# Inverse of a chunk's triangular matrix: its 16x16 blocks on VectorE by way of DRAM, decay rows by DMA, and four gate pairs ahead of the merge

## The reference, cut to what matters

```python
diff = G[..., :, None] - G[..., None, :]            # G: cumulated log decay
decay = jnp.where(tri_incl, jnp.exp(jnp.where(tri_incl, diff, 0.0)), 0.0)
a_mat = jnp.where(tri_strict, beta[..., None] * kk * decay, 0.0)
sol = lax.linalg.triangular_solve(a_mat + eye, rhs, left_side=True, lower=True, unit_diagonal=True)
...
s = (einsum(q, k) * scale + cum[:, :, q0:q1, None] - cum[:, :, None, :q1])   # forgetting attention
...
merged = sigmoid(gate_a) * y_a + sigmoid(gate_b) * y_b
```

## Time and profile before

| | |
|---|---|
| median of 3 runs | 2027.18 us (2027.12 to 2027.74) |
| the profiled execution | 2026.91 us |
| its span | 2025.1 us, 28477 instructions |
| mean granted TensorE clock | 0.993 of full |
| TensorE busy (matmul) | 1969.9 us (97%) |
| TensorE weight load | 1607.0 us (79%) |
| VectorE | 904.0 us (45%) |
| ScalarE | 692.0 us (34%) |
| GpSimd | 929.7 us (46%) |
| DMA queue of SP | 171.21 MB, 26.1% of 16 engines |

### The profile page before, as it was taken

The page is one execution under the profiler, slowest core; times in us unless marked ns, Lnnn a source line. Parts: engine busy times, 40 slices in busy tenths (PEclk is TensorE's granted clock), DMA queues, the critical chain, the costliest instruction groups (busy, mean ns, idle before and its releaser), DMA issues.

```text
span 2025.1 us, 28477 instructions
## 1 busy us (share of the span) xinstructions
PE 1969.9 (97%) x10484; PEld 1607.0 (79%) x10484; DVE 904.0 (45%) x1566; ACT 692.0 (34%) x1390; POOL 929.7 (46%) x711
## 2 busy tenths in 40 slices
PE   6999999999989999999999999999999999999997
PEld 5788778877768888888888788888778888888886
DVE  4766776677642122221212356667432235335143
ACT  4343333433342223332324344455332232222122
POOL 3443354434424456445445534234244555546455
PEclk9999999999999999999999999999999999999998
DMA  5111111111113252323233322121232323323232
GB/s 188 63 63 62 52 41 62 62 52 52 63 42 114 83 180 91 106 91 98 93 97 101 107 92 73 48 75 64 63 126 93 104 82 102 108 84 96 93 103 73
DMA packets 50645, 174.25 MB, mean 86 GB/s; under 512 B 6544, under 2 KB 7312, under 8 KB 50320
## 3 DMA queue, kind: packets, MB, share of 16 engines
q1 hardware_dynamic: 50432, 171.21, 26.1%
q10 hardware_dynamic: 144, 2.10, 0.3%
HBM read 169.09 MB, written 4.19 MB: 86 GB/s over the span
## 4 chain that ended last, share of the span: by engine, by line
PE 91%; DVE 5%; issue 2%; ACT 1%; DMA 0%; POOL 0%; DVEq 0%; POOLq 0%; ACTq 0%; SPq 0%
PE bank L284 26%; PE bank L286 26%; PE bank L285 26%; PE bank L1491 2%; PE bank L1480 2%; PE bank L1474 2%; PE bank L950 1%; PE bank L1671 1%; PE bank L934 1%; PE bank L1658 1%; PE bank L920 1%; DVE branch_a_lo L546 0%; DVE decay_b L1969 0%; DVE branch_b_lo L546 0%; PE bank L1557 0%
## 5 line engine op out<-in xcount | busy, mean ns | idle before, releaser
L273 POOL TENSOR_TENSOR slab_lo<-slab_raw,slab_hi 128x512 fp32r<-128x512 f32 x604 | 822.4, 1387 | 995.9 <-ACT slab_hi L266 995.8
L284 PE MATMUL bank<-u_hi,slab_hi 128*128 128x512 f32 x1584 | 656.8, 415 | 18.3 <-POOL slab_lo L273 13.5
L286 PE MATMUL bank<-u_hi,slab_lo 128*128 128x512 f32 x1584 | 620.9, 392 | 0.0
L285 PE MATMUL bank<-u_lo,slab_hi 128*128 128x512 f32 x1584 | 619.6, 391 | 0.0
L266 ACT CAST slab_hi<-slab_raw 128x1024 fp32r<-128x1024 f32 x302 | 313.8, 1045 | 230.8 <-PE bank L286 229.7
L284 PEld LDWEIGHTS bank<-u_hi,slab_hi 128*128 128x128 f32 x1584 | 299.2, 189 | 79.9 <-issue 18.3
L286 PEld LDWEIGHTS bank<-u_hi,slab_lo 128*128 128x128 f32 x1584 | 298.3, 188 | 64.9
L285 PEld LDWEIGHTS bank<-u_lo,slab_hi 128*128 128x128 f32 x1584 | 299.6, 189 | 53.7 <-issue 1.7
L284 PE MATMUL bank<-hidden_hi,slab_hi 128*128 128x512 f32 x432 | 168.4, 390 | 0.3
L286 PE MATMUL bank<-hidden_hi,slab_lo 128*128 128x512 f32 x432 | 168.1, 389 | 0.0
L285 PE MATMUL bank<-hidden_lo,slab_hi 128*128 128x512 f32 x432 | 168.1, 389 | 0.0
(11 more groups left out here) (336 smaller groups left out, 2669.6 us busy)
## 6 DMA issues: line engine op xcount, KB each, us to landing
slab_raw<-slabs SPq DMA_DIRECT2D x302, 512.0 KB, 3.4
residual<-x_t SPq DMA_DIRECT2D x2, 1024.0 KB, 7.1
x_tok<-x SPq DMA_DIRECT2D x1, 2048.0 KB, 13.5
residual<-x_t SPq DMA_DIRECT2D x1, 2048.0 KB, 8.8
residual_store<-residual SPq DMA_DIRECT2D x1, 2048.0 KB, 8.8
residual<-residual_store ACTq DMA_DIRECT2D x1, 2048.0 KB, 8.2
out_t<-residual SPq DMA_DIRECT2D x8, 256.0 KB, 2.1
cos_ret<-cos_r SPq DMA_DIRECT2D x1, 256.0 KB, 4.0
```

The costliest lines, as they stand in the source:

```text
L273: ins = pool.tensor_tensor(w_lo[s][:, ks, :], raw[s][:, ks, :], w_hi[s][:, ks, :].bitcast(F32), ALU.subtract)
L284: pe.matmul(bank, w_hi[s][:, k, :], x_hi[:, k, :], start=first, stop=False)
L285: pe.matmul(bank, w_hi[s][:, k, :], x_lo[:, k, :], start=False, stop=False)
L286: mm = pe.matmul(bank, w_lo[s][:, k, :], x_hi[:, k, :], start=False, stop=last)
```

## The change

The levels b = 1, 2, 4 and 8 leave TensorE. a_t is now the whole product of 128x512; SP stores it to DRAM with a row pitch such that the 32 diagonal blocks of 16x16 can be read back one to a partition (`blocks_out`). A new token `zb` on VectorE inverts the blocks there, in 19 instructions on 32 partitions (`product` multiplies elementwise with broadcast operands and sums). SP stores the result, and after that reads it back as zi (`blocks_back`), which `xt` transposes. `Y0`/`X0` to `Y2`/`X2` are what were levels 4 to 6. GpSimd makes the two masks left in one token `am`, now 128x512 each. `zb` stands after `vp`, and `kpd` waits for it, since k_rhs is its scratch. `gr` and `cr` go: the table of cumulated sums is transposed once in the first round (`gates3`), stored to DRAM, and SP loads two rows for each head, broadcast to all partitions (`load_rows`). AHEAD becomes 4: LAST holds eight gate slabs, six spread between the tokens and two behind them, and the split of the branches (`br0`..`br7`) stands between the parts of those two. Homes of the eight gate tiles move to the residual's place and others.

```diff
-LEVELS = 7
+SB = 16
+SUBS = T // SB
+DIAG = SB * (SB + 1)
+LEVELS = (16, 32)
 HB, QB = 64, 32
 HW = NT * HB
 SCALE = float(P) ** -0.5
 SLOTS = 4
-DVE_STEPS, LATE_STEPS = 26, 10
+DVE_STEPS, LATE_STEPS = 38, 10
 LEAD = 2
 
-AHEAD = 2
+AHEAD, SPREAD = 4, 6
...
+    row_store = nc.dram_tensor("row_store", (2 * HEADS * NT, P), F32, kind="Internal").ap()
+    row_view = row_store.rearrange("(a h n) t -> h a (n t)", a=2, h=HEADS)
+    pitch = (P // SB) * SB * (P + 1)
+    a_store, z_store = [nc.dram_tensor(f"{x}_blocks_store", (NT * pitch,), F32, kind="Internal").ap() for x in "az"]
+
+    def tiles_in(store):
+        return store.rearrange("(n x) -> n x", n=NT)[:, 0:P * P].rearrange("n (p c) -> p n c", p=P)
+
+    def blocks_in(store):
+        return store.rearrange("(q x) -> q x", q=SUBS)[:, 0:SB * P].rearrange("q (i w) -> q i w", w=P)[:, :, 0:SB]
...
+        g_line, cumr = rows[:, 0, :], rows[:, 1, :]
...
+        gates_ahead = [g[:] for g in gate_home] + [q[:, 3:3 + T] for q in rawq] + [a_out[:], raw_fq[:]]
...
-        ORDER = """gr cr fvt s0.0 dif s0.1 colb fr bd s0.2 eg fk s0.3 kk th3 s0.4 S0 s0.5 z0 s0.6 xt sl3 E0 s0.7 dm qk s1.0 Y1
-                   e0 s1.1 tv P0 s1.2 vp s1.3 s1.4 X1 kpd T0 S1 s1.5 E1 s1.6 Y2 qd P1 s1.7 O0 s2.0 X2 e1 T1 S2 s2.1
-                   E2 cv0.0 s2.2 Y3 O1 s2.3 cv0.1 P2 X3 s2.4 cv0.2 s2.5 Y4 T2 s2.6 S3 cv0.3 s2.7 X4 E3 s3.0 e2 O2 s3.1 Y5
-                   th0 P3 s3.2 cv1.0 s3.3 X5 T3 cv1.1 s3.4 sl0 s3.5 Y6 O3 cv1.2 s3.6 tq s3.7 X6 cv1.3 s4.0 e3 s4.1 vk
+        ORDER = """fvt s0.0 dif s0.1 colb fr bd s0.2 eg fk s0.3 kk th3 s0.4 S0 s0.5 am s0.6 sl3 E0 s0.7 dm qk s1.0
+                   e0 s1.1 tv P0 s1.2 vp zb s1.3 s1.4 kpd T0 S1 s1.5 E1 s1.6 qd P1 s1.7 O0 s2.0 e1 T1 S2 s2.1
+                   E2 cv0.0 s2.2 O1 s2.3 xt cv0.1 P2 s2.4 cv0.2 s2.5 Y0 T2 s2.6 S3 cv0.3 s2.7 X0 E3 s3.0 e2 O2 s3.1 Y1
+                   th0 P3 s3.2 cv1.0 s3.3 X1 T3 cv1.1 s3.4 sl0 s3.5 Y2 O3 cv1.2 s3.6 tq s3.7 X2 cv1.3 s4.0 e3 s4.1 vk
...
-                if (places.index(n) + 1) * 2 * AHEAD * KT // len(places) > part:
+                if (places.index(n) + 1) * SPREAD * KT // len(places) > part:
...
+        LAST.append(f"e{SPREAD - 1}")
+        for g in range((2 * AHEAD - SPREAD) * KT):
+            j, t = SPREAD + g // KT, g % KT
+            LAST.append(f"s{j}.{t}")
+            if t == 0 and j > SPREAD:
+                LAST.append(f"e{j - 1}")
+            if g % 2 == 0:
+                LAST.append(f"br{g // 2}")
...
+        def branch_lo(dve, rnd, k):
+            if k == 0:
+                if rnd == 0:
+                    dve.wait_ge(sem("oa"), HEADS)
+                    dve.wait_ge(sem("ob"), HEADS)
+                else:
+                    dve.wait_ge(sem("ret_out"), 2 * RET_HEADS)
+                    dve.wait_ge(sem("att_out"), 2 * RET_HEADS + 1)
+                dve.tensor_scalar(ms_col[:, 0:1], ms_col[:, 0:1], 1.0, None, ALU.mult).then_inc(sem("branches_done"), 1)
+            for n, (hi, lo, br) in enumerate(((a_hi, a_lo, br_a), (b_hi, b_lo, br_b))):
+                dve.wait_ge(sem("br_hi"), (rnd * KT + k) * 2 + n + 1)
+                dve.tensor_tensor(lo[:, k, :], br[:, k, :], hi[:, k, :].bitcast(F32), ALU.subtract)\
+                    .then_inc(sem("br_lo"), 1)
...
+            def blocks_out(c):
+                sp.wait_ge(sem("masked"), c + 1)
+                sp.wait_ge(sem("blocks_moved"), 80 * c + 32)
+                sp.dma_start(tiles_in(a_store), c4(a_t[:])).then_inc(sem("blocks_moved"), 16)
+                sp.wait_ge(sem("blocks_moved"), 80 * c + 48)
+                sp.dma_start(sub_u[:, 0:SB * SB].rearrange("q (i j) -> q i j", j=SB), blocks_in(a_store))\
+                    .then_inc(sem("blocks_moved"), 16)
+
+            def blocks_back(c):
+                sp.wait_ge(sem("sub_z"), c + 1)
+                sp.dma_start(blocks_in(z_store), sub_z[:, 0:SB * SB].rearrange("q (i j) -> q i j", j=SB))\
+                    .then_inc(sem("blocks_moved"), 16)
+                sp.wait_ge(sem("blocks_moved"), 80 * c + 80)
+                for r in (0, HB):
+                    sp.dma_start(c4(zi[r:r + HB, :]), tiles_in(z_store)[r:r + HB, :, r:r + HB])\
+                        .then_inc(sem("blocks_moved"), 16)
+
+            sp.wait_ge(sem("mhalf"), 1)
+            sp.dma_start(z_store[0:P * T].rearrange("(p t) -> p t", t=T), zeros[:]).then_inc(sem("blocks_moved"), 16)
+            sp.dma_start(z_store[P * T:].rearrange("(p t) -> p t", t=T), zeros[0:1, :]).then_inc(sem("blocks_moved"), 16)
+
+            def load_rows(i):
+                sp.wait_ge(sem("exp"), 4 * i)
+                sp.dma_start(rows[:], row_view[bass.ds(i, 1), :, :].to_broadcast([P, 2, T])).then_inc(sem("rows_landed"), 16)
...
+                            if ph is ph_heads and j == 5:
+                                blocks_out(i - 1)
+                            if ph is ph_heads and j == 6:
+                                blocks_back(i - 1)
+                                load_rows(i)
...
-                def gr():
-                    pe.wait_ge(sem("head_cols"), c + 1)
-                    rows_of(bB, h_small[:, Q_GCUM, :]).then_inc(sem("g_row_ps"), 1)
-
-                def cr():
-                    pe.wait_ge(sem("sq"), 4 * c + 4)
-                    rows_of(bD, h_small[:, Q_LFC, :]).then_inc(sem("cum_row_ps"), 1)
+                def gates3():
+                    pe.wait_ge(sem("gl_cols"), 1)
+                    pe.transpose(bA[0:2 * HEADS * NT, 0:P], gl_cols[:], ident[:]).then_inc(sem("gl_ps"), 1)
...
-                    if l < LEVELS - 1:
-                        pe.wait_ge(sem("atm"), 6 * c + l + 1)
-                    if l == 1:
-                        pe.wait_ge(sem("x0"), c + 1)
-                    else:
-                        pe.wait_ge(sem("x_new"), 5 * c + l - 1)
-                    if l < LEVELS - 1:
-                        quads(bA, atm[l % 2], xi).then_inc(sem("y_ps"), 1)
-                        return
+                    if l < len(LEVELS):
+                        pe.wait_ge(sem("atm"), 2 * c + l + 1)
+                    pe.wait_ge(sem("x_new"), 3 * c + l + 1)
                     pe.sem_inc(sem("level_begun"), 1)
                     for n in range(NT):
                         q = slice(n * HB, (n + 1) * HB)
-                        mm = pe.matmul(bA[HI, q], a_off[LO, q], xi[LO, q], start=True, stop=True)
+                        if l < len(LEVELS):
+                            for r in (LO, HI):
+                                mm = pe.matmul(bA[r, q], atm[l][r, n * P + r.start:n * P + r.stop], xi[r, q],
+                                               start=True, stop=True)
+                        else:
+                            mm = pe.matmul(bA[HI, q], a_t[LO, n * P + HB:(n + 1) * P], xi[LO, q], start=True, stop=True)
                     mm.then_inc(sem("y_ps"), 1)
...
+                    pe.wait_ge(sem("y"), 3 * c + l + 1)
+                    if l == 0:
                         pe.wait_ge(sem("v_rhs"), c + 1)
-                    if l > 1:
-                        pe.wait_ge(sem("z_new"), 6 * c + l - 1)
-                    if l < LEVELS - 1:
-                        quads(bC, yi, zi).then_inc(sem("zy_ps"), 1)
-                        return
+                    else:
+                        pe.wait_ge(sem("z_new"), 3 * c + l)
                     pe.sem_inc(sem("level_begun"), 1)
                     for n in range(NT):
-                        mm = pe.matmul(bC[LO, n * HB:(n + 1) * HB], yi[HI, n * HB:(n + 1) * HB],
-                                       zf[HI, n * P + HB:(n + 1) * P], start=True, stop=True)
+                        q = slice(n * HB, (n + 1) * HB)
+                        if l < len(LEVELS):
+                            for r in (LO, HI):
+                                mm = pe.matmul(bC[r, q], yi[r, q], zi[r, q], start=True, stop=True)
+                        else:
+                            mm = pe.matmul(bC[LO, q], yi[HI, q], zf[HI, n * P + HB:(n + 1) * P], start=True, stop=True)
                     mm.then_inc(sem("zy_ps"), 1)
...
-                    dve.wait_ge(sem("g_row_ps"), c + 1)
+                    dve.wait_ge(sem("rows_landed"), 16 * c + 16)
                     for n in range(NT):
                         q = slice(n * P, (n + 1) * P)
-                        ins = dve.tensor_scalar(dt_[:, q], bB[:, q], h_small[:, Q_GCUM, n:n + 1], 0.0, ALU.subtract,
+                        ins = dve.tensor_scalar(dt_[:, q], g_line[:, q], h_small[:, Q_GCUM, n:n + 1], 0.0, ALU.subtract,
                                                 ALU.min)
...
                 def kpd():
                     dve.wait_ge(sem("sq_ps"), 4 * c + S_K + 1)
+                    dve.wait_ge(sem("sub_z"), c + 1)
...
-                    for out_, p0, c0 in ((a_c, 0, 0), (a_c, HB, HB), (a_off, 0, HB)):
-                        p_, c_ = slice(p0, p0 + HB), slice(c0, c0 + HB)
```

(69 more changed lines are left out.)

139 lines of the change are left out of this document (69 added, 70 removed).

## The result

The changed kernel takes 2039.05 us (median of 5 runs), the kernel before 2027.12 in the runs beside it: a ratio of 1.0056 (95% interval 1.0041 to 1.0071), slower by 0.6%. One of the five took 3252.16 us at a mean granted clock of 0.557; the ratio leaves it out, and the median of the other four is 2038.1. The profiled execution took 2037.12 us.

The account below looks back on a forecast made before the run. TensorE, busy for 97% of the span, was taken to bound the kernel. Seven rounds at +1.85 us (+13.0) and the last round's -4.9 gave +8.1 on the median 2027.18: 2035.3 us, range 2008 to 2057.

Parts of the forecast that it names:

- leaves TensorE, a round: TensorE's queue: six inverse stages a head (4.6 us) and eight transposes (0.89 us) go, together 5.5 us a round.
- (a): VectorE from kk to vp: zb's turn comes 8.6 us after kk, bounds 8.0 to 9.2.
- (b): Transfers into zb: blocks land 5.6 us after kk, 8.8 at the slab's price; costed at nothing.
- (c): zb on VectorE: 19 instructions on 32 partitions take 5.7 us, bounds 4.0 and 7.0.
- (d): Behind zb on VectorE: kpd gives k_rhs 15.6 us after kk, so TensorE waits 4.1 us at O0.
- (e): TensorE at T1: it needs P1 from VectorE, a second wait of 1.6 us.
- (f): Granted clock: after the gaps it falls from 2.4 to 1.2 GHz once each round, 1.6 us lost.
- wait at kk: TensorE at kk, for VectorE's decay_b: the new kk keeps its small wait of 0.37 us.
- last round and merge: Last head's round, gate slabs and merge: 88.6 us against 93.5, so 4.9 us gained.
- Rival A: VectorE reaches kpd sooner, zb takes 4.0 us, the clock holds: faster, 2004 us; chance 0.27.
- B: Block transfers through DRAM are late, 5.6 us in each of eight heads: 2080 us; chance 0.13.
- C: New waits eat the 5.5 us and the last round's gain is small: within 4 us of 2027; chance 0.12.

Follow-up runs that it names:

- e1: Changed kernel with zb reduced to one small copy, the block inverse left out, transfers and order kept: 1981.64 us, ratio 0.9774.
- e2: Changed kernel with zb working on a constant tile and waiting for no transfer, all transfers still made: 2038.14 us, ratio 1.0052.
- e5: Changed kernel with twenty unread 128x128 products of constant tiles in TensorE's idle stretch ahead of O0: 2032.27 us, ratio 1.0024.
- e3: Changed kernel with zb's scratch in the tile of squares and kpd ahead of zb on VectorE: 2040.29 us, ratio 1.0063.
- e6: Changed kernel with zb cut into nine pieces, k_rhs early, other VectorE steps reordered and levels begun later: 2013.01 us, ratio 0.9932.
- e8: Against e6: second and third rows' steps earlier, decay mask, silu and convolution later, levels three slab steps later: 2027.80 us, ratio 1.0001.

## Why the prediction was right, and where its sizes were off

The forecast (VectorE's order makes TensorE wait at O0, and a spell of the lower clock comes with it) is what the trace shows: 2039.05 us against 2035, and the profiled execution grew by 2037.12 - 2026.91 = 10.2 us where the sum had 8.1. Term by term:

| step | forecast | measured |
|---|---|---|
| leaves TensorE, a round | 5.45 | 5.43 (e1) |
| (a) zb's turn after kk | 8.6 | 8.67 |
| (b) wait for the trips | 0 | 0 (e2) |
| (c) zb | 5.7 | 6.4 |
| (d) wait at O0 | 4.1 | 5.2 (16.5 - 11.3) |
| (e) wait at T1 at full clock | 1.6 | 1.27 (e5) |
| (f) lower clock | 1.6 | 1.16 (after less e5) |
| wait for raw_z | not named | 0.43 |
| wait at T2 at full clock | not named | 0.50 (e5) |
| wait at kk | stays at 0.37 | 0 |
| a settled round | +1.85 | +2.66 |
| seven rounds | +13.0 | +17.9 |
| last round and merge | -4.9 | -7.7 |

The measured terms add to 2.8 for a settled round. The seven intervals from kk to kk differ by 1.75 us in the first and 2.7 in the fifth and sixth; the seventh, 3.5, already ends inside the last round.

The mechanism held. Two things in it were not as told. T1's wait and the clock overlap: the forecast adds 1.6 and 1.6, but in the changed kernel T1 waits only 0.32, since TensorE reaches it later at the lower clock; the split in the table is e5's. And kk's small wait was to stay and is gone. The term that was mis-sized is (c). The seven small steps (1.1 us) and the eight 64-element ones (1.7) came as summed; of the four with 512 elements the two reductions took 0.68 and the two products 1.00 and 1.06, where I had 0.68 from k_dec for all. The products read both operands through views that repeat or stride, with four dimensions, on 32 partitions; k_dec reads a bank as it lies and repeats only its other operand. No run here separates this from other causes. This makes 0.7 us of zb. With O0 possible 0.2 us sooner and k_rhs ready at 16.4 instead of 15.6 us after kk the wait is 1.1 longer. The Trainium skill's formula (VectorE: DVE Perf Modes, the section on the errata of SBUF-source operations) gives 0.69 us for 512 elements, an estimate: it fits k_dec and the reductions (0.68), and neither product. The estimate of 1.8 us by it for the eight short ones and my 1.6 lie about as far from the measured 1.7.

The last round gained 7.7 us instead of 4.9, since two waits that I had put there, 1.0 at kk and 1.0 for later ones, didn't come (0.2 in all), T1's was 0.3 and not 1.7, against an O0 wait of 6.1 and not 4.6. That is 6.6 us of waits for 8.3, so 1.7 of the 2.8; no run assigns the other 1.1, and the split of the sum by kk, which puts the last round's start into the seven intervals, blurs it. The two errors partly cancel, so the total is nearer than its parts, which is luck. The three gaps in the merge are there as forecast; the first of them in the timeline of PE of the changed kernel:

```profile
630.96 0.47 PE L295 MATMUL bank<-branch_a_hi,slab_hi 128*128 128x512 f32 x1 [0.83 <-issue]
```

The others follow at 642.93 and 654.92.

Rival A was wrong by zb's length (6.4 us, where it needed 3.9 or 5.5), B by e2 (trip out) and by xt without a wait (trip back), C by the same terms as A. "kpd can't go ahead: k_rhs is zb's scratch" was true and beside the point, as e3 shows: P1 stood behind zb as well.

## What to carry to other kernels

Work moved off the bounding engine is worth what its new place in the other engine's queue lets through: here 5.4 us a round left TensorE, and 6.4 us in one piece on an engine that is idle for 29% of the round took 7.4 back (68.20 against 60.78); cut into nine pieces between the steps of a chain that TensorE waits for, the same work took 1.55 (62.33; the order of the other steps differs too). Moving one neighbour (e3) only moves the wait, and pieces in the wrong places (e6, e8) bring others and can bring the lower clock back, so place every piece by the time at which its reader comes. Two engines that write side by side want a look too: where they meet, 0.17 us became 1.26.
